# The output's split one turn later, and the softmax divisors of two heads as one reciprocal on VectorE and one copy on GpSimd

## What is computed

```python
def gqa_blocked(q, k, v):
    ...
    def one_block(qblk):
        s = jnp.einsum("bkgqd,bksd->bkgqs", qblk, k).astype(jnp.float32) * scale
        p = jax.nn.softmax(s, axis=-1).astype(v.dtype)
        return jnp.einsum("bkgqs,bksd->bkgqd", p, v)
...
def parallel_mixer(h, w_in, ...):
    ...
    a = dwconv_centred(a, conv_dw, conv_dw_b)
    ...
    att = gqa_blocked(q, k, v)
    mixed = jnp.concatenate([a, att], axis=-1)
    return jnp.einsum("bsc,cd->bsd", mixed, w_out)
```

## Time and profile before

| | us |
|---|---|
| median of 3 runs | 2682.43 |
| lowest and highest of them | 2680.8, 2686.41 |
| the profiled execution, time | 2686.31 |
| the profiled execution, span of the core | 2684.7 |
| TensorE busy in it | 2594.7 |
| VectorE busy in it | 1243.8 |
| ScalarE busy in it | 935.8 |
| GpSimd busy in it | 622.2 |

### The profile page before, as it was taken

One profiled execution on the slowest core, in us unless ns is written; L12 is line 12 of the kernel. 1 busy time (PEld: TensorE's weight loads), 2 busy tenths in 40 slices (PEclk: granted clock), 3 DMA queues, 4 the chain that ended last, 5 costly groups with the idle time before them and its releaser, 6 DMA issues.

```text
span 2684.7 us, 29010 instructions
## 1 busy us (share of the span) xinstructions
PE 2594.7 (97%) x11787; PEld 2115.7 (79%) x11787; DVE 1243.8 (46%) x1628; ACT 935.8 (35%) x1376; POOL 622.2 (23%) x467
## 2 busy tenths in 40 slices
PE   8898979999999999999999999999998999999999
PEld 6766767788877788888888888888887787788887
DVE  7886455655633433335333333333335555533322
ACT  4465334444422332224323222322223444332221
POOL 4654220322211422101222101222001332222200
PEclk9977989999999999999999999999998999999999
DMA  4210221232222233222223322333221111233222
GB/s 163 71 40 16 94 79 48 71 101 95 94 91 83 85 98 101 89 94 81 94 94 99 96 92 94 100 101 93 93 95 53 42 47 33 87 105 100 92 95 88
DMA packets 67060, 227.28 MB, mean 85 GB/s; under 512 B 7280, under 2 KB 8816, under 8 KB 66928
## 3 DMA queue, kind: packets, MB, share of 16 engines
q1 hardware_dynamic: 66928, 225.44, 26.4%
HBM read 223.31 MB, written 2.10 MB: 84 GB/s over the span
## 4 chain that ended last, share of the span: by engine, by line
PE 87%; DVE 8%; issue 2%; ACT 2%; POOL 1%; DMA 0%; SPq 0%; DVEq 0%; POOLq 0%; ACTq 0%
PE main L374 19%; PE main L376 19%; PE main L375 19%; PE score L374 6%; PE score L376 6%; PE score L375 6%; PE out L374 3%; PE out L376 3%; PE out L375 3%; DVE cv L580 1%; DVE wl L366 1%; DVE tmp L1255 1%; DVE hxl L494 1%; PE turn L442 1%; PE turn L441 1%
## 5 line engine op out<-in xcount | busy, mean ns | idle before, releaser
L366 DVE TENSOR_TENSOR wl<-raw,wh 128x1024 fp32r<-128x1024 f32 (+2 forms) x435 | 564.5, 1300 | 837.1 <-ACT wh L358 836.7
L358 ACT ACTIVATE wh<-raw 128x1024 fp32r<-128x1024 f32 (+2 forms) x435 | 441.1, 1017 | 633.9 <-PE main L376 524.8
L374 PE MATMUL main<-hxh,wh 128*128 128x512 f32 x1264 | 498.5, 394 | 27.0 <-DVE mv_l L1107 14.5
L375 PE MATMUL main<-hxl,wh 128*128 128x512 f32 x1264 | 494.3, 391 | 0.0
L376 PE MATMUL main<-hxh,wl 128*128 128x512 f32 x1264 | 494.2, 391 | 0.0
L374 PE MATMUL main<-hh,wh 128*128 128x512 f32 x880 | 347.7, 395 | 0.7 <-POOL hl L1496 0.5
L376 PE MATMUL main<-hh,wl 128*128 128x512 f32 x880 | 347.5, 395 | 0.0
L375 PE MATMUL main<-hl,wh 128*128 128x512 f32 x880 | 347.5, 395 | 0.0
L374 PEld LDWEIGHTS main<-hxh,wh 128*128 128x128 f32 x1264 | 238.9, 189 | 84.1 <-DVE mv_l L1107 14.9
L376 PEld LDWEIGHTS main<-hxh,wl 128*128 128x128 f32 x1264 | 238.7, 189 | 50.3
L375 PEld LDWEIGHTS main<-hxl,wh 128*128 128x128 f32 x1264 | 238.8, 189 | 48.7
(11 more groups left out here) (376 smaller groups left out, 3511.7 us busy)
## 6 DMA issues: line engine op xcount, KB each, us to landing
raw<-in_wts SPq DMA_DIRECT2D x371, 512.0 KB, 3.6
raw<-in_wts SPq DMA_DIRECT2D x52, 384.0 KB, 3.0
raw<-in_wts SPq DMA_DIRECT2D x12, 256.0 KB, 2.6
x<-in_xT SPq DMA_DIRECT2D x4, 512.0 KB, 7.9
out<-x SPq DMA_DIRECT2D x8, 256.0 KB, 3.8
memx<-in_memT SPq DMA_DIRECT2D x1, 1024.0 KB, 8.6
band<-in_pool SPq DMA_DIRECT2D x1, 768.0 KB, 4.4
rope<-in_rope SPq DMA_DIRECT2D x1, 512.0 KB, 6.3
```

The lines of the kernel that those rows point to most:

```text
L358: e.activation(wh[i % NCONV][:, 0:n], raw[i % NRAW][:, 0:n], ACT.Copy).then_inc(*sig.up("weight_high", ("high", i)))
L366: e.tensor_tensor(wl[i % NCONV][:, 0:n], raw[i % NRAW][:, 0:n], f(wh[i % NCONV][:, 0:n]), ALU.subtract) \
L374: e.matmul(o, ah, bh, start=start, stop=False)
L375: e.matmul(o, ah, bl, start=False, stop=False)
```

## The change

The new `soft(n)` puts the small numbers of a pair's two heads into one slot of `stat`, 16 columns each. VectorE makes one reciprocal for a pair, over 2 x 4 numbers, in the first transposing turn of the pair's second head; GpSimd makes one copy that spreads all eight over the 512 columns, in the same turn ahead of its tap, into a tile of its own (`divide_turn`, the fifth `tmp` tile). ScalarE's `value_scalar` and GpSimd's `value_gpsimd` move from the turn after the pair's last transposed block to the turn after that (`ended` in place of `before`), on ScalarE also from behind the tap to ahead of it. `value_vector` stays where it is. The loops of these two engines get one turn more.

```diff
+        divide_turn = Ring(tmp_slots[4:5])
...
+        def soft(n):
+
+            j, g = HEADS[n]
+            return stats.of(("soft", j))[:, 16 * g:16 * g + 16]
...
-            if i == 0:
-                _, old = stats.take(("soft", n))
-                e.wait_ge(*sig.at(old))
-            c = stats.of(("soft", n))
+            j, g = HEADS[n]
+            if i == 0 and g == 0:
+                _, old = stats.take(("soft", j))
+                e.wait_ge(*sig.at(old))
+            c = soft(n)
...
-        def divisors_vector(e, n):
-            j, g = HEADS[n]
-            c = stats.of(("soft", n))
-            e.wait_ge(*sig.at(("exp", 4 * n + 3)))
-            e.reciprocal(c[:, 12:16], c[:, 8:12]).then_inc(*sig.up("reciprocal", ("recip", n)))
-            if g == 0:
-                _, old = att_turn.take(("divide", j))
-                e.wait_ge(*sig.at(old))
-            sx = att_turn.of(("divide", j))
-            e.wait_ge(*sig.at(("recip", n)))
-            e.tensor_copy(sx[:, :].rearrange("p (i g c) -> p i g c", i=4, g=2)[:, :, g, :], c[:, 12:16].unsqueeze(2).broadcast_to([P, 4, 64])) \
-                .then_inc(*sig.up("divisor", ("divisor", n), ("free", ("soft", n))))
+        def divisors_vector(e, j):
+            st = stats.of(("soft", j))[:, 0:32].rearrange("p (g c) -> p g c", g=2)
+            e.wait_ge(*sig.at(("exp", 8 * j + 7)))
+            e.reciprocal(st[:, :, 12:16], st[:, :, 8:12]).then_inc(*sig.up("reciprocal", ("recip", j)))
+
+        def divisors_gpsimd(e, j):
+
+            sx, old = divide_turn.take(("divide", j))
+            st = stats.of(("soft", j))[:, 0:32].rearrange("p (g c) -> p g c", g=2)
+            e.wait_ge(*sig.at(old))
+            e.wait_ge(*sig.at(("recip", j)))
+            e.tensor_copy(sx[:, :].rearrange("p (i g c) -> p i g c", i=4, g=2),
+                          st[:, :, 12:16].rearrange("p g i -> p i g").unsqueeze(3).broadcast_to([P, 4, 2, 64])) \
+                .then_inc(*sig.up("divisor", ("divisor", j), ("free", ("soft", j))))
...
-            for t in range(TURNS + 6):
-                now, before = value_turn(t), value_turn(t - 1)
+            for t in range(TURNS + 7):
+                now, ended = value_turn(t), value_turn(t - 2)
                 if 0 < t <= TURNS:
                     mix_exp_scalar(e, t - 1)
                 if now:
                     value_split_scalar(e, *now)
                     if now[1] == 3 and now[0] % 2 == 1:
                         divisor_rows_scalar(e, now[0] // 2)
+                if ended and ended[1] == 3 and ended[0] % 2 == 1:
+                    value_scalar(e, ended[0] // 2)
                 tap_scalar(e, k)
-                if before and before[1] == 3 and before[0] % 2 == 1:
-                    value_scalar(e, before[0] // 2)
...
-                    if now[1] == 0:
-                        divisors_vector(e, now[0])
+                    if now[1] == 0 and now[0] % 2 == 1:
+                        divisors_vector(e, now[0] // 2)
...
-            for t in range(TURNS + 6):
-                before = value_turn(t - 1)
+            for t in range(TURNS + 7):
+                now, ended = value_turn(t), value_turn(t - 2)
+                if now and now[1] == 0 and now[0] % 2 == 1:
+                    divisors_gpsimd(e, now[0] // 2)
                 tap_gpsimd(e, k)
-                if before and before[1] == 3 and before[0] % 2 == 1:
-                    value_gpsimd(e, before[0] // 2)
+                if ended and ended[1] == 3 and ended[0] % 2 == 1:
+                    value_gpsimd(e, ended[0] // 2)
```

More of the change, by code:

```diff
@@ L953, in value_split_vector @@
                 .then_inc(*sig.up("p_low", ("ptl", n, m), ("free", ("pt", n, m))))
-        def divisors_vector(e, n):
-            j, g = HEADS[n]
-            c = stats.of(("soft", n))
-            e.wait_ge(*sig.at(("exp", 4 * n + 3)))
-            e.reciprocal(c[:, 12:16], c[:, 8:12]).then_inc(*sig.up("reciprocal", ("recip", n)))
-            if g == 0:
-                _, old = att_turn.take(("divide", j))
-                e.wait_ge(*sig.at(old))
-            sx = att_turn.of(("divide", j))
-            e.wait_ge(*sig.at(("recip", n)))
-            e.tensor_copy(sx[:, :].rearrange("p (i g c) -> p i g c", i=4, g=2)[:, :, g, :], c[:, 12:16].unsqueeze(2).broadcast_to([P, 4, 64])) \
-                .then_inc(*sig.up("divisor", ("divisor", n), ("free", ("soft", n))))
+        def divisors_vector(e, j):
[10 more added lines that the diff above has]
+                .then_inc(*sig.up("divisor", ("divisor", j), ("free", ("soft", j))))
         def divisor_rows_tensor(e, j):
             b, old = mainb.take(("drows", j))
-            sx = att_turn.of(("divide", j))
+            sx = divide_turn.of(("divide", j))
             e.wait_ge(*sig.at(old))
-            e.wait_ge(*sig.at(("divisor", 2 * j + 1)))
+            e.wait_ge(*sig.at(("divisor", j)))
             for i in range(4):
```

## The result

| | us |
|---|---|
| changed kernel, median of 6 runs (lowest, highest) | 2672.97 (2669.17, 2675.34) |
| kernel before on the same chip, median of 6 (lowest, highest) | 2684.21 (2680.78, 2689.44) |
| ratio, with its 95% interval | 0.9956 (0.9938 to 0.9974) |
| profiled execution of the changed kernel, time and span | 2672.47, 2670.9 |

The change saves about 11 us of the 19.3 forecast. The lines of code have moved: L937 is now the exponential (was L930), L945 the transposes of the probabilities (L938), L959 the low part (L952), L965 the one reciprocal, L973 the copy on GpSimd, L1010 the division (L1001), L1016 the output's high part (L1007), L581 and L600 the taps (L580, L599).

What follows compares the result with a forecast made beforehand. VectorE sets the attention's pace at full clock; pair-end waits drop TensorE to half clock. Pace 42.2, waits 3.0 and sharing 2.0 against 66.48 save 19.3 us: 2686.3 to 2667.0 (2663.1 from the median), range 2655 to 2681.

Steps and rivals of the forecast that it cites:

- The split a turn later: ScalarE at pair ends: exponential runs ahead of L1007, removing 2.46 of TensorE's 2.47 us wait at 177.48.
- What is late next: Pair ends: value product waits for VectorE's low part, 0 to 1.5 us, taken as 1.0; three cost 3.0.
- The sign of being wrong: Attention: a value product waits 1.4 us for the low part and products of 0.79 us follow.
- Rival 1: Clock falls again at some pair ends: one fall 2671.6 us (chance 0.17), two falls 2680.1 (0.12).
- The divisors: Fewer reciprocals and copies on VectorE, copies on GpSimd: balance nothing, between +3.3 and -0.3 us.
- The sum: 17 attention turns: 42.2 us pace, 3.0 waits, 2.0 sharing make 47.2 against 66.48, 19.3 us less.
- Sharing: VectorE and GpSimd taps wait for each other: 2.60 us a turn instead of 2.48, 2.0 more over 17 turns.
- one fall: Clock falls at one pair end: 10.8 us saved, time 2671.6, chance 0.17.
- clock held: Full clock through the attention's pair ends: by itself 2655 to 2666 us, chance 0.55.
- two low stretches: Attention's two long low-clock stretches with the turns at their edges: 8.5 us each of the 19.3 saved.
- Rival 2: Odd heads' turns: GpSimd's copy holds VectorE's tap, the wait reaches 1.38 us, clock falls: 2688.5 us, chance 0.08.
- Rival 3: ScalarE's wait for the division only moves, pair ends cost TensorE the same: 2682 us, chance 0.08.

Runs made afterwards that it cites:

- divisors_only: Changed kernel with the splits put back in their turn of before, one reciprocal and one GpSimd copy a pair kept: 2681.86 us, ratio 0.9989 to the kernel before.
- late_only: Kernel before with only the ScalarE and GpSimd splits moved a turn later, VectorE's eight reciprocals and copies kept: 2677.90 us, ratio 0.9978.
- again: Changed kernel run once more, unaltered, with a second profile: 2670.06 us, ratio 0.9944 to the kernel before.
- new_3: Changed kernel run a third time, unaltered: 2673.28 us, ratio 0.9961 to the kernel before.
- old_again: Kernel before, unaltered, run once more for a second profile: 2683.87 us, one run.
- copy_on_vector: Changed kernel with the pair's one spreading copy on VectorE behind its reciprocal instead of on GpSimd: 2678.82 us, ratio 0.9984 to the kernel before.
- old_filled: Kernel before with eight useless TensorE products ahead of each of the three score products that waited: 2677.38 us, ratio 0.9969.
- new_filled: Changed kernel with five useless TensorE products ahead of each of the three waiting value products: 2667.41 us, ratio 0.9942 to the kernel before.
- short_ve_taps: Changed kernel with VectorE's taps from the attention on made over 8 of 512 columns, convolution left incomplete: 2655.64 us, one run.
- after: First profile of the changed kernel, unaltered: profiled execution 2672.47 us.

## Why the prediction was right in its direction and mechanism, and too large

- **The split a turn later: right.** The queue order on ScalarE held TensorE. With the exponential ahead of L1016 no score product waits for it; with the split back in its place (divisors_only) the wait returns with 2.19 us. L1016 itself still waits 1.65 us, a little over the 1.5 that the prediction allowed, and no TensorE instruction waits for it.
- **What is late next: the low part, 1.35 us instead of 1.0.** It lies within the bound of 0 to 1.5, and the case "the tap is held by GpSimd" is the one that holds: VectorE's tap ends at 173.49, behind GpSimd's at 172.94. Three cost 4.05 us instead of 3.0.
- **The sign of being wrong was met.** The prediction named a value product that waits 1.4 us, with products of 0.79 us behind it: 1.36 us with 0.80 in the first profile, 1.38 with 0.79 in the second. That is Rival 1, and it came beside the forecast mechanism, not in its place.
- **The divisors: as costed, nothing by themselves, but not nothing with the split.** The sum put them at zero because it counted VectorE's time alone. With the split moved they decide how late the low part is: late_only waits 1.61 and 1.63 us at two pair ends where the changed kernel waits 1.34 to 1.38, and its median is 7.8 us above again's. The GpSimd copy takes 0.95 us, not 0.70. Nobody waits for it. Left on VectorE it costs 8.8 us of medians against again, on one chip. The page of the Trainium skill that the prediction weighed (Perfetto Trace Analysis, Optimizing Scalar/DVE Operations) says that offloading between these two might not help; here it did.
- **Sharing: real, but it grows by 0.4 us on balance, not 2.0.** The 17 turns of 45.27 us hold two of the waits, the third lies just behind. Without the two (2.69) they take 2.50 each, where 2.60 was forecast and 2.48 had been measured. VectorE lost copies in the same turns, so the 0.4 is not the price of sharing by itself.
- **The sum for that trace: right, in part by luck.** 45.27 + 1.36 = 46.6 us answer to the 47.2, and the output projection starts 20.2 us earlier against 19.3. Waits 1.05 us too small and sharing 1.6 us too large nearly cancel. It is luck too that the median, 2672.97, lies so near the 2671.6 of "one fall": in the first profile (2672.47) the clock held through all 17 turns, and what is missing to the forecast 2667.0 went in the second attention.
- **The step that failed is the first case of the forecast, "clock held", and its size of two low stretches at 8.5 us each, 17.0 together.** The forecast took all low clock of the 17 turns in one profiled execution of before as what the kernel always pays, and none of it as what the changed kernel pays. By the estimate over all executions the clock gives 8.3 us. Both ends were off. Waits of 1.36 to 1.38 us still bring the clock down in the changed kernel, for 3.4 us, 20.5 and 3.4 in its three profiles, and in the third the wait of 0.97 adds 6.8. And the kernel before has fewer falls in other executions (stage 126.1, and times down to 2669.44). The means of the stage are 128.1 (two profiles) and 112.8 (three), 15.3 us apart.
- **Rival 1 was no separate case but a mixture in every run.** It gave 10.8 us for one fall. Its threshold, unknown between 0.97 and 1.38, isn't there: 0.97 was followed by a fall in new_3 and old_again, and 2.19 by none in divisors_only. The argument from one trace to "this long a wait falls, that one doesn't" is what misled.
- **Rival 2** (a new fall in the odd heads' turns, from GpSimd's copy) did not come: in the first profile the longest waits for the low part there are 0.83 us, at 183.64 and 205.13, without a fall. It is the copy on VectorE that makes such a wait and fall (2.32 us in copy_on_vector). **Rival 3** is excluded by the intervals, which end below 1 in all three runs. The chance of 0.76 for "faster" counts 0.04 of mixed cases to which the list of chances gives nothing.
- **Open:** between the stage's 15.3 us and the 11.6 of the whole lie 3.7. The profiled executions themselves show such a difference: their times lie 11.2 us apart on the mean (two of before, three of the changed kernel), 4.1 less than their stages, and 3.3 of it are the second attention. The change doesn't touch that stage. It takes 172.1 and 178.6 us in the profiles of before and 178.7, 178.7 and 178.6 in those of the changed kernel. The longer time is the usual one, with either order of the queues: 178.6 to 178.7 in ten of all fourteen profiles, old_filled among them, and 175.6 in late_only, 175.7 in new_filled, 169.0 in short_ve_taps. With two profiles of before it can't be said how often that kernel has the shorter one. And no run shows what decides whether a wait is followed by a fall.

## What to carry to other kernels

Where a short idle time of TensorE is followed by products at half speed, price the low stretch and not the wait, and look at several executions before you say which wait brings the clock down: one trace gives a sample, not a rule. When a wait in an in-order queue is removed, compute what is late next down to the instruction, and move out of its way what nobody waits for, as the tap ahead of the division here. Price two changes together where both bear on the same queue: here one was worth nothing without the other. A VectorE instruction with long and short records of one shape can be a sign of what GpSimd does beside it; an edit that makes one of them trivial shows the price at once.

## What the runs showed of the hardware

- Idle times of nearly the same length, in the same place of the program, are followed by a fall of the granted clock from 2.4 to 1.2 GHz in one execution and not in the next: 1.35 and 1.38 us at the second pair's end (after, again), 0.97 at the first low part (after, new_3). Within one execution, 2.19 us at one pair's end were followed by a fall and at another's not (divisors_only). Once down, the clock stayed down through turns in which TensorE had no gap (17.0 us in divisors_only, 20.4 in again, 30.0 in old_again).
- Work of no use on TensorE in place of idle time was cheaper than the idle time, though it was longer: 3.62 us of it in place of 2.47, with the kernel at 0.9969 of its time (0.9956 to 0.9982).
- A VectorE instruction of 8 columns takes up to 1121 ns beside a GpSimd instruction of 512 columns, 173 at best.
